# Fetching both expert rows of every pick in one transfer, and making each pick's coefficient alone

## The reference

```python
def chunk(xc):                      # 128 tokens
    q = (xc @ w_q).reshape(C, Hh, 2, half)
    s = jnp.einsum('chpd,hpnd->chpn', q, sub_keys)
    top_s, top_i = lax.top_k(s, K)                  # K = 16, twice for each of 8 heads
    cand = top_s[:, :, 0, :, None] + top_s[:, :, 1, None, :]
    best_s, best_j = lax.top_k(cand.reshape(C, Hh, K * K), K)
    ...
    expert = ia * PEER_KEYS + ib                    # 128 picks per token
    g = jax.nn.softmax(best_s, axis=-1)
    u = u_tab[expert]
    a = jax.nn.gelu(jnp.einsum('cd,chkd->chk', xc, u), approximate=False)
    coeff = g * a
    return jnp.einsum('chk,chkd->cd', coeff, v_tab[expert])
```

## The kernel before

| rows | beside them | v on TensorE | v on VectorE |
|---|---|---|---|
| 0 to 149 | choices (top-k on VectorE) of chunks 0 to 2, memory attention | 1024 columns | none |
| 150 to 299 | in-projection of chunks 3 to 7 (`project_tokens`) | none | 1024 columns |
| 300 to 639 | attention of chunks 3 to 7 (`attend`) | 512 columns | 512 columns |
| 640 to 2047 | memory attention and choices of chunks 3 to 7 | 768 columns | 256 columns |

## Time and profile before

### The profile page before, as it was taken

One profiled execution on the slowest core, in us unless ns is written; L12 is line 12 of the kernel. 1 busy time (PEld: TensorE's weight loads), 2 busy tenths in 40 slices (PEclk: granted clock), 3 DMA queues, 4 the chain that ended last, 5 costly groups with the idle time before them and its releaser, 6 DMA issues.

```text
span 3789.9 us, 34958 instructions
## 1 busy us (share of the span) xinstructions
PE 2933.6 (77%) x8920; PEld 1517.5 (40%) x8920; DVE 2484.4 (66%) x5699; ACT 1298.0 (34%) x3333; POOL 1420.4 (37%) x1367
## 2 busy tenths in 40 slices
PE   8797866984886598989689797787878777766665
PEld 6655533431443355555344343333333333322222
DVE  0321218786876477767437888877887887788765
ACT  1212312221121244444234544444443454344333
POOL 0000003443776376657423333333333333333332
PEclk9897888997898799999899999999989999999999
DMA  7844156777998999999889999999999999999998
GB/s 298 274 147 184 57 215 214 238 263 283 346 338 327 352 369 341 363 352 355 333 318 369 401 411 417 409 414 415 411 407 421 413 405 407 421 410 414 417 411 351
DMA packets 274454, 1297.10 MB, mean 342 GB/s; under 512 B 27888, under 2 KB 63088, under 8 KB 180464
## 3 DMA queue, kind: packets, MB, share of 16 engines
q0 software_dynamic: 195120, 1073.83, 72.2%
q1 hardware_dynamic: 74384, 203.74, 14.4%
q10 hardware_dynamic: 4752, 17.30, 1.2%
HBM read 1231.07 MB, written 63.70 MB: 342 GB/s over the span
## 4 chain that ended last, share of the span: by engine, by line
DMA 31%; issue 7%; DVE 5%; PE 4%; ACT 3%; POOL 0%; POOLq 0%; DVEq 0%; SPq 0%; ACTq 0%
DMA s_ring<-peer_uv,s_expert 17%; DMA e_more_slots<-peer_uv,s_expert 10%; PE e_acc L503 3%; DVE e_part L427 1%; PE e_product L1859 1%; DMA e_more_slots<-peer_v,s_expert 1%; DMA next_h<-e_h 1%; DMA e_h<-norm_ffn_row 1%; DMA s_scratch<-norm_final_row 1%; DVE s_ring L394 1%; ACT L341 1%; ACT s_diagonal L324 0%; ACT s_gate L343 0%; DVE s_dots L394 0%; DVE e_more_slots L394 0%
## 5 line engine op out<-in xcount | busy, mean ns | idle before, releaser
L503 PE MATMUL e_acc<-s_ring,s_diagonal 128*128 128x512 f32 (+1 forms) x2168 | 898.8, 543 | 379.6 <-ACT s_diagonal L324 352.8
L394 DVE CUSTOM_DVE_ANT_0 s_ring<-s_ring,e_x_copy 128x1024 f32<-128x1024 f32 x548 | 666.6, 1217 | 221.9 <-DMA s_ring<-peer_uv,s_expert 215.1
L503 PEld LDWEIGHTS e_acc<-s_ring,s_diagonal 128*128 128x128 f32 x2168 | 396.5, 199 | 943.5 <-ACT s_diagonal L324 587.5
L278 POOL DMA_INDIRECT s_ring<-peer_uv,s_expert x462 | 437.5, 947 | 783.1 <-DVE e_part L427 551.8
L278 POOL DMA_INDIRECT s_ring<-peer_u,s_expert x331 | 377.4, 1140 | 449.9 <-DVE s_expert L1796 230.8
L503 PE MATMUL e_acc<-e_more_slots,s_diagonal 128*128 128x512 f32 (+1 forms) x948 | 387.4, 536 | 153.9 <-ACT s_diagonal L324 146.3
L278 POOL DMA_INDIRECT s_ring<-peer_v,s_expert x325 | 373.2, 1148 | 332.0 <-PE e_acc L503 94.9
L341 ACT ACTIVATE s_dots<-s_dots 128x1 f32<-128x1 f32 x704 | 142.2, 202 | 961.3 <-DVE s_dots L394 959.0
L324 ACT ACTIVATE s_diagonal<-s_ident,s_gate 128x128 f32<-128x128 f32 x949 | 371.2, 399 | 223.0 <-PE e_acc L503 100.1
L278 POOL DMA_INDIRECT e_more_slots<-peer_uv,s_expert x231 | 217.6, 942 | 413.8 <-DVE e_part L427 273.5
L394 DVE CUSTOM_DVE_ANT_0 s_ring<-s_ring,s_x 128x1024 f32<-128x1024 f32 x245 | 299.5, 1222 | 104.6 <-DMA s_ring<-peer_u,s_expert 69.2
(11 more groups left out here) (233 smaller groups left out, 3618.5 us busy)
## 6 DMA issues: line engine op xcount, KB each, us to landing
w_in_kept<-w_in SPq DMA_DIRECT2D x8, 1104.0 KB, 11.8
w_in_gained<-w_in_kept SPq DMA_DIRECT2D x8, 1104.0 KB, 10.2
p_w_in<-w_in_gained SPq DMA_DIRECT2D x8, 1104.0 KB, 19.0
f_w_big<-w_mem_kv SPq DMA_DIRECT2D x4, 2048.0 KB, 19.2
f_w_big<-peer_w_q_t SPq DMA_DIRECT2D x2, 4096.0 KB, 17.9
peer_scores<-f_stage_s SPq DMA_DIRECT2D x16, 512.0 KB, 8.5
e_mem_scores<-mem_scores SPq DMA_DIRECT2D x2, 4096.0 KB, 14.6
e_mem_values<-mem_values SPq DMA_DIRECT2D x2, 4096.0 KB, 25.0
```

The source lines that it names most:

```text
L278: pool.indirect_dma_start(out=to, out_offset=None, in_=table, in_offset=bass.IndirectOffsetOnAxis(ap=self.expert[c % PICK_BUFFERS][:, k:k ...
L394: dve.tensor_tensor_reduce(row, row, x[:, :], 1.0, 0.0, ALU.mult, ALU.add, self.dots[:, k:k + 1]).then_inc(self.u_used, 1)
L503: last = pe.matmul(self.acc[:, at:to], self.diagonal[:, made % DIAGONALS, :], row[:, at:to], start=(n == group[0]), stop=(n == group[-1]))
```

## The change

All 1024 picks come as pairs from `peer_uv`, from the first on: `ROWS` is u0, v0, u1, v1 and so on, with no lead of u over v and no drain. The rows at which the stages end stay as they are, so each stage moves as many bytes as before; of the 86 u tiles and 64 v tiles of the first stage there are now 75 and 75. Slots are handed out in pairs, and a pair is free when its u and its v are used. Beside the ring of 8 (4 pairs) the first stage gets 2 more slots, the second 6, the third none and the last 4, as it had.

Gelu and coefficient are made pick by pick for all picks (`coeff_alone`), in all stages, at the pick's place in ScalarE's queue; `GELU_AT` and `COEFF_AT`, with their operations on 16 columns, are gone. In `project_tokens` two more calls of `stream.scalar` are added, ahead of parts 3 and 6. VectorE adds its share of V one pick behind: the add of pick g stands behind the dot of pick g + 1. At the end of a chunk in the stages with mode "split" the four closing steps stand two rows later. The choices of chunk 0 end at row 46, not 45.

```diff
-LEAD = 22
-PAIRS_FROM = 331
-ALONE_FROM = PAIRS_FROM // TOPK * TOPK
-ROWS = [("u", g) for g in range(LEAD)]
-for _g in range(PAIRS_FROM - LEAD):
-    ROWS += [("u", LEAD + _g), ("v", _g)]
-ROWS += [("v", g) for g in range(PAIRS_FROM - LEAD, PAIRS_FROM)]
-PAIRS_AT = len(ROWS)
-for _g in range(PAIRS_FROM, TOTAL_PICKS):
-    ROWS += [("u", _g), ("v", _g)]
+ROWS = [(kind, g) for g in range(TOTAL_PICKS) for kind in "uv"]
...
+            if n == start:
+                free = [slot for slot in free if slot < RING]
+            if n == start + RING:
+                free = list(range(RING, RING + self.extra[s], 2)) + free
+                last_in = {slot: m for slot, m in last_in.items() if slot < RING}
+            if kind == "u":
+                slot = free.pop(0)
...
     def gpsimd(self, until):
-            for m in {self.before[n], self.before[n + 1] if paired else None} - {None}:
...
+            before = self.before[n]
+            if before is not None:
+                pool.wait_ge(self.u_used, ROWS[before][1] + 1)
+                if self.pe_columns(before + 1) > 0:
+                    pool.wait_ge(self.v_pe, self.pe_through[before + 1])
+                if self.pe_columns(before + 1) < D:
+                    pool.wait_ge(self.v_dve, self.dve_through[before + 1])
...
     def scalar(self, until):
-            if n in GELU_AT:
-                i = GELU_AT[n]
-                h = i % PEER_HEADS
-                at = slice(TOPK * h, TOPK * (h + 1))
-                act.wait_ge(self.u_used, TOPK * (i + 1))
-                act.activation(self.active[:, at], self.dots[:, at], ACT.Gelu).then_inc(self.activated, 1)
...
-            if kind == "v" and self.pe_columns(n) > 0:
-                if g >= ALONE_FROM:
-                    self.coeff_alone(g)
...
+            if kind == "v":
+                self.coeff_alone(g)
+                if self.pe_columns(n) > 0:
+                    made = self.pe_through[n]
+                    need(act, self.v_pe, made - DIAGONALS)
+                    act.activation(self.diagonal[:, made % DIAGONALS, :], self.ident[:, :], ACT.Copy,
+                                   scale=self.coeff(g)).then_inc(self.diagonal_ready, 1)
...
     def vector(self, until):
-            if n in COEFF_AT:
...
-                dve.tensor_tensor(gate, self.active[:, at], gate, ALU.mult).then_inc(self.coeff_ready, 1)
...
             elif self.pe_columns(n) < D:
+                first, end, mode = self.stages[self.stage_of[n]]
+                add = self.add_to_h if mode == "split" else self.add_part
+                if n - 2 >= first:
+                    add(n - 2)
+                if n == end - 1:
+                    add(n)
...
+    def add_to_h(self, n):
+        dve = self.nc.vector
+        g = ROWS[n][1]
+        rest = slice(self.pe_columns(n), D)
+        self.wait_row(dve, n)
+        dve.wait_ge(self.coeff_made, g + 1)
+        self.wait_h(g // PICKS, self.dve_through[n] - 1)
+        dve.scalar_tensor_tensor(self.h[:, rest], self.row(n)[:, rest], self.coeff(g), self.h[:, rest], ALU.mult,
+                                 ALU.add).then_inc(self.v_dve, 1)
...
 def project_tokens(nc, io, first, end, ahead=None, keep=None, stream=None, until=0):
+            stream.more_slots = sb("p_more_slots", [P, stream.extra[1], D])
...
                 if more:
                     square_x(t + 1)
+                if woven:
+                    beside(stream.scalar, t, 3)
+                if more:
                     keep_x_t(t + 1)
...
+                if woven:
+                    beside(stream.scalar, t, 6)
                 act.wait_ge(q_turned, t + 1)
...
-FIRST_CHOICES = [45, 100, 150]
+FIRST_CHOICES = [46, 100, 150]
-STAGES = [(PICK_FIRST, "pe", D), (PROJECT_REST, "split", 0), (ATTEND_REST, "split", BANK), (len(ROWS), "pe", 3 * D // 4)]
+STAGES = [(PICK_FIRST, "pe", D, 2), (PROJECT_REST, "split", 0, 6), (ATTEND_REST, "split", BANK, 0), (len(ROWS), "pe", 3 * D // 4, 4)]
```

115 lines of the change are left out of this document (34 added, 81 removed).

## The result

The changed kernel takes 3995.2 us (median of 4 runs, 3988.91 to 3998.95) against 3799.88 us for the kernel before (4 runs, 3793.36 to 3814.47): a ratio of 1.049, 95% interval 1.046 to 1.053, so 4.9% slower. The forecast was slower, with 3923 us; the measured time lies at the upper end of the range of 3860 to 3995, 0.2 us over it, and 30 us over the forecast's own range. So the direction and the main cause were foreseen, and about a third of the loss was not.

A forecast was written before the change was run, and what follows sets the result against it. Each stage has its own limit: VectorE first, VectorE and DMA second, TensorE and DMA in the attention, DMA last. 126 - 5 + 4 + 0 = 125 us on a 3789.9 us span gave a 3923 us median, range 3860 to 3995.

The forecast's parts named there:

- rival B: Attention, projection units: ring of four pairs too short, a pair every 4.4 us, 72 us more, 3995; chance 0.12.
- the long gaps: Attention: eight gaps between exponentials, each over 10 us, 106.5 us in all; a gap longer than its loop keeps its length.
- The loop of the attention: Attention: two table loads per unit stand in the TensorE-ScalarE loop, stretching 67 ordinary gaps; 126 us more, 90 to 175.
- The projection units: Attention, four units holding the projection: bound by transfers, cost nothing if four pairs in flight are enough.
- First stage: First stage: 11 fewer dots save 13 us, 8 taken back for added loads: -5, between -15 and +20.
- Crossing: Between stages: counted together with the last stage, worth 0, give or take 10 us.
- Second stage: Second stage: 23 us of new waits behind gelus, 19 us of tile waits gained: +4, between -19 and +25.
- Last stage: Last stage: DMA keeps its pace, 11 more dots hide behind it; worth 0, give or take 10 us.
- D: Attention: bound by DMA and GpSimd, loads not in the loop, so DMA gains and it is faster, 3740; chance 0.06.
- E: Attention: slack in the long gaps pays for most, within 0.5% of before; chance 0.03.
- F: Attention: a table switch holds ScalarE longer than the load shows, 174 us more, 4097; chance 0.05.
- C: First two stages: coupling of engines per pick costs its upper ends, 20 + 25, 3969; chance 0.12.

The follow-up runs named there:

- gelus alone: Kernel before, with gelu and coefficient made pick by pick, V still 22 picks behind u, single transfers kept, two added ScalarE calls in the in-projection: 3962.95 us, 1.046.
- Three pairs: Changed kernel with three pairs of slots in the attention in place of four: 4114.69 us, 1.086.
- five pairs: Changed kernel with five pairs of slots in the attention in place of four, and one mask-table buffer in place of three: 3999.32 us, 1.054.
- loads alone: Kernel before, with one more one-column gelu on ScalarE in each attention unit, adding only table switches: 3859.04 us, 1.018.
- the exponential first: Changed kernel; in the attention ScalarE takes the next unit's exponential before the picks' coefficients, TensorE the picks after the next turn: 3944.34 us, 1.042.

## Why the prediction was right, and where it was short

The direction and the term that decides were right for the reason given. That the range held the time is in part luck: its upper end was the forecast plus the 72 us of rival B. The forecast was 72 us short indeed, but 50 of them lie where B had them, and by a cause that is at most in part B's; the others come from terms that the sum had at nothing or as a gain, less what the long gaps gave back.

**The loop of the attention: right, to its size.** The loads went from 24 to 159 (136 more were counted), ScalarE to 504 us (over 480), TensorE's share from 0.88 to 0.80, not to 0.73, DMA's to 0.78 (below 0.85), and the exponentials span 729 us (about 700). Among the ordinary units with one and two picks the shortest gaps are 5.7 and 7.1 us at 4 blocks, 6.7 and 7.6 at 7, and 7.9 at 8 (two picks), where the loops were 5.8 and 6.7, 6.9 and 7.8, and 8.0. The kernel with gelus alone lengthened the 67 ordinary gaps by 126.8 us; the step said 126. In the changed kernel itself they grew by 149.3, the four projection units by 50.5, and the eight long gaps shrank by 38.4; the step had all the lengthening in the ordinary ones. So an arithmetic of starts from one timeline, with each added instruction put into the chain, gave the cost of a change that no trace showed.

**The projection units: the step that failed.** The prediction let them "cost nothing if four pairs in flight are enough" and kept the other case as rival B, 72 us at a chance of 0.12. They cost 50.5 us. Between gelus alone and the changed kernel lie the pairs, V right behind its own dot, and TensorE's picks with it. The attention grows by 39.1 us there: 47.8 in the projection units and 22.5 in the ordinary ones, less 31.1 in the long gaps. Part of the shift is no loss: the wait at the change of chunk (a gap of 18.4 us before, a few units on) now falls into the third projection unit, 47.4 us long. VectorE's timeline in the last one shows what the picks there wait for, a dot each time its tile has landed:

```profile
1928.82 1.23 DVE L365 CUSTOM_DVE_ANT_0 s_ring<-s_ring,s_x 128x1024 f32<-128x1024 f32 x1 [0.43 <-DMA s_ring<-peer_uv,s_expert]
...
1932.24 1.23 DVE L365 CUSTOM_DVE_ANT_0 s_ring<-s_ring,s_x 128x1024 f32<-128x1024 f32 x1 [1.52 <-DMA s_ring<-peer_uv,s_expert]
...
1936.92 1.23 DVE L365 CUSTOM_DVE_ANT_0 s_ring<-s_ring,s_x 128x1024 f32<-128x1024 f32 x1 [2.78 <-DMA s_ring<-peer_uv,s_expert]
...
1939.53 1.23 DVE L365 CUSTOM_DVE_ANT_0 s_ring<-s_ring,s_x 128x1024 f32<-128x1024 f32 x1 [0.70 <-DMA s_ring<-peer_uv,s_expert]
...
1943.52 1.23 DVE L365 CUSTOM_DVE_ANT_0 s_ring<-s_ring,s_x 128x1024 f32<-128x1024 f32 x1 [2.10 <-DMA s_ring<-peer_uv,s_expert]
```

and GpSimd's, the issues of the third, fourth and fifth of these tiles:

```profile
1931.19 0.94 POOL L265 DMA_INDIRECT s_ring<-peer_uv,s_expert  x1 [5.67 <-DVE s_h L384]
1933.76 1.19 POOL L265 DMA_INDIRECT s_ring<-peer_uv,s_expert  x1 [1.64 <-issue]
1935.48 0.94 POOL L265 DMA_INDIRECT s_ring<-peer_uv,s_expert  x1 [0.53 <-issue]
```

From issue to dot pass 5.7, 5.8 and 8.0 us, and a pick comes every (1943.52 - 1928.82) / 4 = 3.7 us. Rival B had asked for landings under 6.6 us or it would cost, and for up to 12.1 us at 4.4 a pick: the truth is at the border. Three pairs (+107) show that the depth matters below four; five pairs show that more of it gives next to nothing, though VectorE then waits for tiles hardly longer than before the change. It is not the loads either: without them the four units take 140.8 us, 44.2 over before. What these runs leave is that V comes right behind its own dot, with TensorE's picks between the products of the projection, as in the first stage, and TensorE at its lower clock. No run separates these two or takes them from the pairs, so the cause of the 50 us stays open.

**First stage: the wrong sign.** The step took 8 of 13 us back, -5 with a range up to +20; it came out at +18. Its cause was named wrongly too. It feared the 15 more loads; 19 gelu loads and 11 at the choices' exponentials are there now, and taking the gelus' loads away gives 3 us. "Against it stand 11 more V products on TensorE, which has slack (262 of 366 us), and the tie of each coefficient to the dot just before": the tie, put at nothing, was the larger cost. The dots did save their 12 us of VectorE's work, and 27 us of waits for TensorE's products came in their place. Moving TensorE two picks back gives 11 us. With coefficients made alone, and V still 22 picks behind, rows 0 to 148 are 8 us longer than before, and these waits 12.9 us. A mean share (262 of 366 us busy) hid that TensorE's products are due at set points.

**Crossing: put at 0, came out at +8.6.** VectorE's longest wait there is for the sine table of the in-projection, before and in the changed kernel:

```profile
DVE s_ring L394 <- DMA p_sin<-sin: 18.7, 1, 18.7
```

```profile
DVE s_ring L365 <- DMA p_sin<-sin: 26.0, 1, 26.0
```

It was 18.6 us in both kernels made from before, 20.2 without the added slots, and 26.1 to 26.2 in others that have them. So this wait grows by 6 us with the slots. The crossing as a whole does not follow it: it is 44.2 us without the slots and 44.5 to 48.5 with them, against 39.2 to 40.0 in the kernel before and those made from it. Some 5 us of it thus come with neither the slots nor the gelus alone, and by what path stays open.

**Second stage: right in sum (+1.5, said +4), with its parts confirmed.** Gelus alone cost 24.6 us (said 23), and the pairs with seven in flight give 23.1 back (said 19). VectorE's waits for ScalarE's small steps, said to be 1.5 and 3.0 us a chunk, are 2.2 (p_c_stat) and 3.2 (p_x_stat). But the giving is the added slots' (35 us), not that of the halved issues, which the step named first.

**Last stage and rivals.** Its pace did not change (-1.2 us). D fell: the load stands in the loop. E fell with it. F fell: had each switch held the engine for longer than the record shows, the loads alone could not have cost 0.5 us each. The Trainium skill (ScalarE: Activation LUTs, "What ACT_TABLE_LOAD costs") has a drain of 1.38 us at each load; the trace shows 0.01 to 0.02 us on either side of it, here again, and the measurement decides. C had its first half (+18 of +20) for another reason than loads, and not its second.

**Sum.** On the path without the 8.1 us ahead of row 0: predicted 126 - 5 + 4 = 125, measured 188.9. The gap of 64 is 35 in the attention, 23 in the first stage, 9 in the crossing and 5 from the last dots of the second stage to the first exponential, less 2.5 in the second stage and 5.9 behind the attention. With the 8.1 us ahead of row 0, which are no cost of the change, these make the 72 us by which the forecast was short.

## What to carry to other kernels

When a function that shares an engine with another is moved from once a batch to once an item, price it in the loop that the engine's queue forms with its neighbours, start to start from a timeline; shares of busy time said that 259 us would fit. When an item's second half is tied to its first, look at every in-order queue that the second half passes, and ask what stands behind it: in the first stage that cost more than the extra instructions did, and a change of order took 11 us of it back. Halving the number of transfers and doubling their size halves how many are in flight unless slots are added: in the second stage four pairs were 12 us slower than single rows (in a kernel that also kept V 22 picks behind), and seven were 23 us faster.

## What the runs showed of the hardware

A table load is 1283 ns each time, with 0.03 us around it where ScalarE waits for nothing else, also when 159 stand in 729 us.

TensorE's granted clock was lower in the kernels in which it waited more. Over the attention, with 2172 to 2182 matmuls each time: 0.94 before (busy 503 of 567 us), 0.92 with loads alone (535 of 636), 0.89 with gelus alone (561 of 690), 0.87 in the changed kernel (580 of 729), 0.82 with three pairs (640 of 836). The order isn't strict: the exponential first has 0.87 as well, at 561 of 678. The engine thus looks busier by up to 137 us at equal work. That is why its share came out at 0.80, where 0.73 was predicted from the work of before. Where the loop sets the pace no run shows a cost of it; in the last projection unit with five pairs TensorE was busy for 32.1 of 34.0 us.
